# Stick-breaking attention: value products of two units in one block in every second unit, closings of banks in the units between

## The reference, cut to what matters

```python
z = jnp.einsum('bqhd,bkhd->bhqk', qb, k) * scale
log_beta = jax.nn.log_sigmoid(z)
log_1mb = jnp.where(strict, jax.nn.log_sigmoid(-z), 0.0)
later = lax.cumsum(log_1mb, axis=3, reverse=True) - log_1mb
a = jnp.where(strict, jnp.exp(log_beta + later), 0.0)
return jnp.einsum('bhqk,bkhd->bqhd', a, v)
...
s_out = rmsnorm(s_out, sb_norm_g[layer])
```

## Time and profile before

| | us |
|---|---|
| median of 3 runs | 2804.65 (2802.63 to 2809.13) |
| profiled execution, its own time | 2805.57 |
| its span, first to last instruction | 2803.8 |
| PE busy | 2745.9 (98%) |
| DVE busy | 1915.7 (68%) |
| ACT busy | 1480.0 (53%) |
| POOL busy | 671.3 (24%) |

### The profile page before, as it was taken

How to read it: one execution, slowest core, us unless ns; L and a number is a source line. 1 busy time by engine, 2 the same in 40 slices (tenths; PEclk the granted TensorE clock), 3 DMA queues, 4 the chain that set the end, 5 groups by cost and what they waited for, 6 DMA issues and landing times.

```text
span 2803.8 us, 51433 instructions
## 1 busy us (share of the span) xinstructions
PE 2745.9 (98%) x19064; PEld 2451.8 (87%) x19064; DVE 1915.7 (68%) x2799; ACT 1480.0 (53%) x2572; POOL 671.3 (24%) x772
## 2 busy tenths in 40 slices
PE   7999999999999999999999999999999999999998
PEld 6888888878888888888899989997889998999886
DVE  6214540078888888886687877876488878877656
ACT  6113221177777777776455555554355555655444
POOL 1832222056776333312011221111100000011110
PEclk9999999999999999999999999999999999999999
DMA  5478997566555542423489999998657775899884
GB/s 198 135 196 208 216 227 193 135 160 144 120 136 124 136 117 56 116 99 98 144 264 326 322 250 307 281 307 256 171 180 245 250 239 153 264 327 302 249 231 156
DMA packets 311734, 563.58 MB, mean 201 GB/s; under 512 B 32480, under 2 KB 78560, under 8 KB 310368
## 3 DMA queue, kind: packets, MB, share of 16 engines
q1 hardware_dynamic: 271168, 467.25, 52.7%
q0 software_dynamic: 39072, 92.30, 17.8%
q10 hardware_dynamic: 1312, 1.64, 0.2%
HBM read 454.11 MB, written 197.13 MB: 232 GB/s over the span
## 4 chain that ended last, share of the span: by engine, by line
PE 71%; DVE 4%; ACT 1%; issue 1%; DMA 1%; POOL 1%; SPq 0%; DVEq 0%; ACTq 0%; POOLq 0%
PE f_ps L2530 28%; PE f_ps L2414 19%; PE h_z L725 5%; PE h_o L1030 4%; PE h_z L728 4%; PE h_z L1011 4%; PE h_o L967 3%; PE h_z L952 2%; DVE f_wlo L1903 1%; DVE h_work L1291 1%; DVE h_negmax L1204 1%; PE f_ps L2454 1%; PE f_ps L2440 0%; DVE f_xsum L2116 0%; DMA f_piece<-act_scratch 0%
## 5 line engine op out<-in xcount | busy, mean ns | idle before, releaser
L1903 DVE TENSOR_TENSOR f_wlo<-f_wraw,f_whi 128x512 fp32r<-128x512 f32 x834 | 574.1, 689 | 234.6 <-ACT f_whi L1896 233.3
L1896 ACT ACTIVATE f_whi<-f_wraw 128x512 fp32r<-128x512 f32 x834 | 520.8, 627 | 394.9 <-PE f_ps L2530 255.5
L2530 PE MATMUL f_ps<-f_hi_s,f_whi 128*128 128x256 f32 x1408 | 391.2, 278 | 7.8 <-DVE f_up L2255 7.8
L2530 PE MATMUL f_ps<-f_lo_s,f_whi 128*128 128x256 f32 x1408 | 391.7, 278 | 0.0
L2530 PE MATMUL f_ps<-f_hi_s,f_wlo 128*128 128x256 f32 x1408 | 389.8, 277 | 0.0
L2530 PE MATMUL f_ps<-f_hi_a,f_whi 128*128 128x256 f32 x1056 | 292.1, 277 | 1.5 <-DVE f_second L2255 1.5
L2530 PE MATMUL f_ps<-f_hi_a,f_wlo 128*128 128x256 f32 x1056 | 291.7, 276 | 0.0
L2530 PE MATMUL f_ps<-f_lo_a,f_whi 128*128 128x256 f32 x1056 | 291.6, 276 | 0.0
L2530 PEld LDWEIGHTS f_ps<-f_hi_s,f_whi 128*128 128x128 f32 x1408 | 264.4, 188 | 9.5 <-DVE f_up L2255 4.9
L1291 DVE TENSOR_TENSOR_SCAN h_work<-h_more 128x1024 f32<-128x1024 f32 (+7 forms) x128 | 249.3, 1973 | 25.8 <-PE h_z L1011 24.7
L2530 PEld LDWEIGHTS f_ps<-f_hi_s,f_wlo 128*128 128x128 f32 x1408 | 264.8, 188 | 0.0
(11 more groups left out here) (213 smaller groups left out, 6195.2 us busy)
## 6 DMA issues: line engine op xcount, KB each, us to landing
f_wraw<-in_w_stream SPq DMA_DIRECT2D x394, 256.0 KB, 4.3
f_wraw<-sums_scratch SPq DMA_DIRECT2D x352, 256.0 KB, 4.9
sums_scratch<-in_w_stream POOLq DMA_DIRECT2D x132, 256.0 KB, 5.6
act_scratch<-f_act SPq DMA_DIRECT2D x88, 256.0 KB, 3.9
combined_acts<-f_act SPq DMA_DIRECT2D x88, 256.0 KB, 5.0
f_wraw<-down_sums SPq DMA_DIRECT2D x88, 256.0 KB, 3.4
f_piece<-combined_acts SPq DMA_DIRECT2D x88, 256.0 KB, 3.2
down_sums<-in_w_stream POOLq DMA_DIRECT2D x66, 256.0 KB, 6.3
```

Of the source, the lines that this page charges most:

```text
L1896: act.activation(w_hi[ring][:], w_raw[ring][:], ACT.Copy).then_inc(S["hi_split"], 1)
L1903: dve.tensor_tensor(w_lo[ring][:], w_raw[ring][:], w_hi[ring][:].bitcast(F32), ALU.subtract).then_inc(S["lo_split"], 1)
L2530: mm = pe.matmul(outs[i], w[ring][:, col], a[name][:, c, :], start=(c == 0 and m == 0), stop=(c == 3 and m == 2))
```

## The change: what it does

A is taken out of the odd units, and an even unit i has A(i-4) and then A(i-3). A closing, which stood in front of A in the unit behind that of its own A, now stands in the odd unit behind the pair of A in which it was applied; sum of squares and norm stand one unit behind that. The line numbers of the changed file below line 831 are one higher.

```diff
-        closing_at = lambda i: pieces[i] if 0 <= i < len(pieces) and pieces[i]["closes"] is not None else None
+        applied_in = lambda i: [pieces[n] for n in (i - 4, i - 3) if 0 <= n < len(pieces)] if i % 2 == 0 else []
+        closing_in = lambda i: [t for t in applied_in(i - 1) if t["closes"] is not None and t is not pieces[-1]]
...
             def breaking(i):
-                cur, turning, applying, closing = piece_at(i), piece_at(i - 2), piece_at(i - 3), closing_at(i - 4)
+                cur, turning = piece_at(i), piece_at(i - 2)
                 for m in range(2):
                     if cur is not None:
                         stick_scores(cur, m)
...
-                if closing is not None:
+                for closing in closing_in(i):
                     lay(closing)
-                if applying is not None:
+                for applying in applied_in(i):
                     stick_apply(applying)
...
             def breaking(i):
-                cur, turning, closing = piece_at(i), piece_at(i - 2), closing_at(i - 4)
-                if closing is not None:
+                cur, turning = piece_at(i), piece_at(i - 2)
+                for closing in closing_in(i):
                     lift(closing)
...
-                if closing is not None:
+                for closing in closing_in(i):
                     settle(closing)
...
-                cur, closed = piece_at(i), closing_at(i - 5)
+                cur = piece_at(i)
...
-                if closed is not None:
+                for closed in closing_in(i - 1):
                     sum_squares(closed)
...
             def breaking(i):
-                closed = closing_at(i - 5)
-                if closed is not None:
+                for closed in closing_in(i - 1):
                     normalize_bank(closed)
```

## The result

The changed kernel takes 2816.90 us (median of 12 runs, 2810.78 to 2826.10) against 2806.62 of the kernel before in the same set (12 runs, 2802.63 to 2814.32). The ratio is 1.0035, with a 95% interval of 1.0025 to 1.0045: 10 us slower, 7 to 13 by the interval. The forecast was 7.8 slower and a median of 2812.5, inside a range of 2801 to 2820. Of the 4.4 between 2812.5 and 2816.90, 2.0 are the kernel before itself, whose median of 12 runs lies above the 2804.65 of the first three.

A forecast was written before the change was run, and what follows sets the result against it. PE, busy 98% of the span, was taken to bound the kernel. Terms of -9.9 + 9.2 + 7.5 + 3 - 1 - 1 = +7.8 us gave a median of 2812.5 us, range 2801 to 2820.

The forecast's parts named there:

- The switches: PE entering and leaving A: merging two A saves 0.30 us a pair, 33 x 0.30 = 9.9 us.
- The loop: First T, scan, gate, even unit's second T: 1.9 us slack gone, mean stall 0.16 us, 2.9 over 18 units.
- Closings: Closings in odd units: ACT's settle delays the gate, 15 x 0.34 plus 1.2 in the first pair, 6.3 us.
- POOL: POOL's norm slows the scan PE waits for, 15 x 0.5 = 7.5 us; value differences add 3; bounds 0 to 18.
- The two ends: Start and end of the stage: 1 us less at each, the end bounded by 0 and 1.5.
- Nothing comes back: Rival: switches saved, loop closes 0.3 us faster, POOL misses the scans that count: -8 us, 2796; chance 12%.
- Break-even: Rival: the loop stalls as computed but POOL falls beside other scans: -1 us, 2804; chance 25%.
- Far slower: Rival: late E holds the next unit's slot, a second 1 us stall per even unit with closing, 2826; chance 6%.

The follow-up runs named there:

- the version with A unmerged: The changed kernel with third gate buffer and settle moved behind the next even unit's gates, but A in every unit again: 0.9982 to the kernel before, 2798.36 us.
- small POOL: The changed kernel with POOL's norm and value differences cut to a few columns (values wrong): 0.9973 to the kernel before; same cut in the kernel before: 0.9975.
- Late settle: The changed kernel, two gate buffers, with settle moved on ACT behind the gates of the next even unit: 1.0005 to the kernel before.
- fastest version: The changed kernel with a third gate buffer and settle moved behind the next even unit's gates: 0.9961 to the kernel before; run again 0.9959, 2793.45 us.
- third buffer: The changed kernel with a third gate buffer, so a gate waits for the scan three steps back: 0.9982; same buffer in the kernel before: 0.9993.
- closings alone: The kernel before with A kept in every unit and only the closings moved to odd units: 0.9998 to the kernel before.

## Why the prediction was right

- **The switches.** 0.30 a pair and 9.9 us were predicted, 0.28 and 9.1 measured by the version with A unmerged (8.2 of stage and 0.9 of stalls). The price came from the chain (1.90 less 1.75, and 0.43 less 0.23) and stood within 10%.
- **The loop.** Predicted stall without closing or POOL: 0.27 in pairs one and three, 0.04 in two and four. Measured in the changed kernel: 0.33 to 0.34 in the first and third (units 6, 8 and 42), 0.23 to 0.24 in the second and fourth (26 and 60). The run with small POOL has more such units: 0.32 to 0.34, and 0.20 to 0.23 in five units of the second and fourth pair. The path was right, the sum some 0.06 short for split scans and 0.16 to 0.20 for plain ones. For the split scores I had added 0.10 on PE's side to every unit of pairs two and four. They cost next to nothing in those five units (2.72 to 2.75 from the second T block of the odd unit to the first of the even one, 2.72 with plain scores) and 0.2 in three others, 20, 24 and 58 (2.90 to 2.95), where they take the stall away: 0.05, 0.01 and 0.01 with small POOL. The bare loop comes to 4.1 in the 17 units without a closing, where 2.9 were predicted for 18.
- **Closings.** 0.74 in the first pair and 0.34 elsewhere were predicted, 6.3 in all. Measured 0.71, then 0.33 to 0.42, and 0.19 to 0.20 at units 28, 62 and 66; with the three units in which POOL is late as well, 7.5, and 5.5 with small POOL. Late settle took 6.2 of the 7.5 away.
- **POOL.** 7.5 and 3 predicted, 9.7 measured (12.8 less 3.1 of stage). Right in sum; the split between norms and value differences isn't measured, since both were cut at once. All 14 norms from unit 11 to unit 67 do meet the first scan of an odd unit, and the longest stalls, 1.93 and 1.65, stand beside value differences. Single stalls of units behind norms are 0.23 to 1.15, of which up to 0.34 are the bare loop, more uneven than the 0.5 that I took for all. The 0.81 of the earlier trace rows was right as a size, but I took the 1.22 beside it for POOL's need, when 0.3 of it is waiting. The Trainium skill (SBUF — State Buffer, Who interferes with whom) has more of this than I used: whoever issues first holds the shared ports for its whole instruction, and the order of issue decides who blocks. The rows agree with it; the section on the hardware below shows how.
- **The two ends.** -1 and -1 predicted, -1.5 and -1.75 measured.
- **Sum.** Stalls of 19.7 predicted, 18.0 measured; +7.8 us predicted, +9.3 in the stage and 10 (7 to 13) in time. By terms: switches 0.8 less saved, the two ends 1.25 better, stalls at T 1.7 less, and 2.4 more of waits for the gate in front of S (weight loads of line 725: 4.3 us in five waits against 1.9 in two), which I had not counted. Those from unit 6 on, 1.56 and 0.64, are in front of the scores of even units 32 and 48, for a gate whose scan the value differences had slowed. With these terms the sum is 8.0. Of the other 1.3, 0.8 lie inside T blocks of units 6 to 66: in a block that had waited, the second transpose starts 0.14 behind the first instead of 0.11. The last 0.5 I can't assign. So the mechanism was right, and that the sum came as near as it did is in part luck: its errors, of 0.8 to 2.4 us each, went both ways.
- **The rivals.** *Nothing comes back* is refuted by the 18.0 us of stalls; with the loop opened and the settle moved, the fastest version comes somewhat below its size (11 us less than before, where -8 was forecast). *Break-even* needed POOL beside other scans; it wasn't. *Far slower* would have shown as stalls in S of odd units of some 15 us; from unit 6 on there were none, and 2.2 us in S of two even units.

What is shown by experiment: that the waits at T cause the loss (third buffer), that of their 18.0 us 8.4 need POOL's work, and 6.2 behind closings the settle ahead of the gate, that closings alone are free, and what merging alone is worth. The bare loop's 4.1 are what is left without POOL in units without a closing, and the third buffer takes these away. What is only read from rows: that the value differences cost more at a time than the norms, since both were cut at once.

## What to carry to other kernels

Before moving work out from between two steps, add up what else ran while it did: each loop over other engines that closes in that time loses its slack, and a loop with 1.9 us of slack shows no wait at all in the profile. The remedy need not be to take the move back; one more buffer on the edge that closes the loop, and the other engine's unhurried work set behind its urgent one, turned 10 us lost into 11 us gained. Not all of the 11 us needs the change: the version with A unmerged is 5 us faster than the kernel before. An operation that is harmless beside a slack instruction (POOL beside the scan) becomes as dear as the critical path when the slack is gone.

## What the runs showed of the hardware

The norm on POOL and the scan on DVE took turns. At 1133.50 the scan was running, and POOL's instruction took 2.44 us, until 0.9 behind the scan's end at about 1135.03; the next part of the scan lost 0.81. Where it began first, 0.14 ahead of a scan, the same instruction took 1.04 and the scan behind it 3.05 instead of 2.27 (unit 23 above); in the earlier trace rows, where it met the last 0.3 us of a scan, 1.22, with the same 0.81 lost behind it. So a scan lost what POOL needed by itself (0.8 to 1.0 us), not POOL's whole row, and only the scan that came second: where POOL waited out a first scan of an odd unit in one piece, that one lost nothing (2.29) and the other head's scan, on which PE doesn't wait, lost it (3.07 from 1036.83 with late settle). A split first scan lost it in its own second part. This is why stalls behind norms were so uneven. I had taken one size for all.

Entering and leaving the 64-column matmuls cost PE 0.28 (A unmerged against merged) to 0.35 us (read from the earlier trace rows) a time at the full clock (1.00 granted), here with transposes in front and scores behind.
